# A two-layer encoder with expert retrieval: three token parts for tile 1, transposed token load, stationary gate weights, tile 0's v slots moved forward

## The chip, the cores and the metric

The kernel runs on one core of a Trainium2 chip. The metric is the device time of one execution in microseconds (us), the median of several.

## What is computed

The input is 256 tokens of 2048 floats. Layer 0 mixes tokens by attention and mLSTM heads that read one projection of the normalised tokens; layer 1 mixes by pooling. Each layer then has a PEER mixer, in which each token picks 128 of 16384 experts. Cut to what matters (`E` stands for the layer's output projection and residual, the routing is left out):

```python
hn = rmsnorm(h, norm_mix_g[layer])            # x * rsqrt(mean(x*x) + eps) * gain
proj = hn @ w_in                              # attention q, k, v; mLSTM q/k, v, output gate; 16 gate columns
# layer 1: pooled = windowed means of hn minus hn; y = pooled @ pool_w * layer_scale
xn = rmsnorm(h, norm_ffn_g[layer])
q = xn @ w_query; expert, gate = top16_of_pairs(q, sub_keys)      # 8 heads x 16 experts a token
act = gelu(einsum('tkd,td->tk', u[expert], xn))                   # 128 dots a token
h = h + einsum('tk,tkd->td', gate * act, v[expert])
```

The output is `rmsnorm(h, norm_f)`. All arithmetic is in float32.

## The kernel before

The tokens are two tiles of 128 (tile 0 and tile 1). Each engine has its own instruction stream, written out by hand, and waits on counting semaphores; so on each engine the order in the text is the order of the work, and a wait holds everything behind it.

**Mixer of layer 0.** SyncE (SP) loads the tokens, gains and constants, then the projection's weights in halves of 2 MiB through three slots (`load_half`). ScalarE (ACT) and VectorE (DVE) normalise a tile into `nrm0`, TensorE (PE) transposes it (`transpose_xn`), both evict it to `xnT`. `straight_half` multiplies `xnT` with a half; after the first half 32 matmuls with 16 moving columns make the gates (L1516), and small steps turn them into decays between the halves. Later halves use `xnT` as the moving operand (L1581).

**PEER, per layer.** The 128 experts of each token have their u rows gathered by GpSimd (POOL), one expert of each of 128 tokens at a time: 128 rows of 8 KiB, 1 MiB, into a ring of buffers (`gather_u`). A ring buffer is free again when VectorE has done its dot (`dot`, L1311: product and sum against the staged tokens in `low`). Tile 0 uses ring `U[0]` (a part of its rows goes to TensorE). Tile 1 is done in two halves of 64 tokens: in a half, the 128 partitions hold 64 tokens twice, with different experts (`idx_p`, made by the copies of L430 from `idx_all`), so each half takes 64 dots. TensorE stages the tokens of a half, doubled, in `low` (`duplicate`, L1823), which VectorE must have finished reading; for the second half this stands in TensorE's stream seven quads before the end of tile 0's spreading.

**From dots to weights.** ScalarE takes the gelu of a half when its dots are done (`gelu_half`, L787), VectorE multiplies with the gates (`weigh_half`, L1337, after the 13th dot of tile 1's fifth group of 16 for the first half), TensorE turns and folds it (`turn_half`). Then, for four tokens at a time (a quad), ScalarE builds two one-hot matrices (`one_hots`, L837 to L846), TensorE multiplies them (`spread`, L1837) and ScalarE copies the result to `W` (`spread_out`, L860). ScalarE does so for the 32 quads of tile 0, then for the 16 of tile 1's first half, both while the dots go on; the last 16 quads have their one-hots made by VectorE (L1370, L1374) after the last dot, and after every two of them TensorE adds one diagonal product of a v gather (`diagonal`, L1845): `ND` = 8 in all.

**v.** Half of v's columns are summed densely: 128 loads of 512 KiB (`load_vd`) against `W` (`dense`, L1858), in the banks of `low`. The other half is gathered: 128 rows of 4 KiB, 512 KiB (`gather_v`, L543), in eight slots. The order of the 256 gathers is the list `gathered`: first `ND` of tile 0, then tile 1 and tile 0 in turns, at the end the last of tile 1. The first 8 gathers go by slot, the next `ND` each wait for a diagonal, the others for VectorE's sums (`add_v`, L1351), which begin when the diagonals are added (`add_diagonals`). `pace` ties the dense loads to the sums.

**The boundary.** When the dense sums are done, SP loads the pooling matrix and its gains (L455, L456). VectorE takes the root of tile 0's norm and scales the pooling matrix with it (`mean_square`, `scale_pooling`, L958) near the end of its sums; TensorE pools tile 0, then tile 1 (L1870), then projects (L1772).

## Time and profile before

| | us |
|---|---|
| median of 3 runs | 3008.47 |
| lowest, highest | 3005.03, 3009.71 |
| the profiled execution | 3007.43 |
| its span in the profile | 3005.6 |

| engine | busy us | share |
|---|---|---|
| TensorE matmul | 2319.2 | 77% |
| VectorE | 2130.7 | 71% |
| ScalarE | 824.9 | 27% |
| GpSimd | 1081.7 | 36% |

DMA moved 1058.78 MB, 352 GB/s over the span. The page gives the mean busy share of the 16 DMA engines in 40 slices of 75 us as digits, tenths of full: `5333235899999999899999969999998999999999`. The first seven slices are the mixer of layer 0, the next sixteen the PEER of layer 0, the rest layer 1. A shares' column says which engine worked, not which one set the end; for that the timelines of one stretch are laid side by side, and in them the bracket behind an instruction tells how long its engine had been idle and what released it. Times in the rows count from the span's start.

### The profile page before, as it was taken

To read this page: it belongs to the slowest core of one execution; us is meant where nothing else is said; L and a number is where in the kernel's file an instruction comes from. 1 tells how busy PE (TensorE), PEld (TensorE's weight loads), DVE (VectorE), ACT (ScalarE), POOL (GpSimd) and SP (SyncE) were. 2 spreads that over 40 slices of the span, in tenths; PEclk is the share of its full clock that TensorE was granted. 3 is DMA by queue.
4 is the path that set the end of the run, shared out by engine and by line. 5 is a ranking of instruction groups with operands and counts; after the bars stand their busy time and mean duration, and the time that the engine had idled before them with its cause. 6 is when DMAs were issued, how large, how long until landed. Compare 5 with 4: busy or idle time off the path is not lost.

```text
span 3005.6 us, 26389 instructions
## 1 busy us (share of the span) xinstructions
PE 2319.2 (77%) x9174; PEld 1707.0 (57%) x9174; DVE 2130.7 (71%) x3110; ACT 824.9 (27%) x2109; POOL 1081.7 (36%) x1028
## 2 busy tenths in 40 slices
PE   8999999778873332799999888788443419999996
PEld 4686545677862332566665557778432316666654
DVE  1242122799999989856666768989998997566667
ACT  1242120112228986100000021212298941000000
POOL 0000000523334333444456624323333334444665
PEclk8999999889985555899999998999755559999998
DMA  5333235899999999899999969999999998999999
GB/s 215 140 112 140 112 116 234 344 413 412 390 389 420 421 416 421 301 410 409 409 409 409 409 265 417 408 411 378 388 421 416 417 420 293 410 409 409 409 409 360
DMA packets 196883, 1058.78 MB, mean 352 GB/s; under 512 B 23952, under 2 KB 24592, under 8 KB 123664
## 3 DMA queue, kind: packets, MB, share of 16 engines
q0 software_dynamic: 147456, 805.37, 66.1%
q1 hardware_dynamic: 49296, 251.74, 21.2%
q8 instruction: 73, 1.20, 0.2%
q14 instruction: 58, 0.48, 0.0%
HBM read 1054.53 MB, written 2.10 MB: 352 GB/s over the span
## 4 chain that ended last, share of the span: by engine, by line
DMA 45%; PE 27%; DVE 20%; issue 3%; POOL 3%; ACT 2%; DVEq 0%; SPq 0%; ACTq 0%; POOLq 0%
DMA arena<-pvg,idx_all 20%; DMA arena<-pu,ints 14%; DVE arena L1311 10%; DMA xnT<-pvg,idx_all 7%; PE bank L1496 7%; DMA arena<-pu,idx_all 4%; PE bank L1581 3%; DVE h L1351 3%; PE bank L1784 3%; PE bank L1733 2%; PE low L1698 2%; PE bank L1791 1%; PE bank L1837 1%; PE low L1687 1%; POOL xnT L543 1%
## 5 line engine op out<-in xcount | busy, mean ns | idle before, releaser
L1311 DVE CUSTOM_DVE_ANT_0 arena<-arena,low 128x2048 f32<-128x2048 f32 x418 | 944.5, 2285 | 93.0 <-DMA arena<-pu,ints 39.9
L1858 PE MATMUL low<-arena 128*128 128x512 f32 x2048 | 901.7, 600 | 31.2 <-DMA arena<-pvd 30.6
L1858 PEld LDWEIGHTS low<-arena 128*128 128x128 f32 x2048 | 601.6, 296 | 331.1 <-DMA arena<-pvd 68.5
L527 POOL DMA_INDIRECT arena<-pu,idx_all x200 | 222.7, 1113 | 862.5 <-DVE idx_all L1280 567.1
L1351 DVE SCALAR_TENSOR_TENSOR h<-arena,cst,h 128x1024 f32<-128x1024 f32 x248 | 318.0, 1285 | 163.8 <-DMA arena<-pvg,idx_all 163.1
L1351 DVE SCALAR_TENSOR_TENSOR h<-xnT,cst,h 128x1024 f32<-128x1024 f32 x248 | 317.6, 1285 | 163.5 <-DMA xnT<-pvg,idx_all 162.3
L1837 PE MATMUL bank<-arena 128*128 128x128 f32 x768 | 194.9, 434 | 294.5 <-ACT arena L846 294.5
L543 POOL DMA_INDIRECT arena<-pvg,idx_all x256 | 280.6, 1096 | 242.9 <-DVE h L1351 177.6
L543 POOL DMA_INDIRECT xnT<-pvg,idx_all x256 | 280.5, 1096 | 238.6 <-DVE h L1351 178.0
L1837 PEld LDWEIGHTS bank<-arena 128*128 128x128 f32 x768 | 167.8, 322 | 322.4 <-ACT arena L846 321.4
L569 ACT ACTIVATE h<-low 128x512 f32<-128x512 f32 x8 | 4.3, 589 | 938.6 <-PE low L1858 938.6
L1784 PE MATMUL bank<-xnT,arena 128*128 128x128 f32 x1792 | 244.7, 288 | 0.0
L837 ACT ACTIVATE arena<-cst,arena 128x128 f32<-128x128 f32 x768 | 233.7, 389 | 0.1
L1784 PEld LDWEIGHTS bank<-xnT,arena 128*128 128x128 f32 x1792 | 231.1, 202 | 0.0
L1733 PE MATMUL bank<-xnT,arena 128*128 128x256 f32 (+1 forms) x1152 | 218.0, 352 | 9.7 <-issue 5.7
L803 ACT ACTIVATE arena<-bank 128x512 f32<-128x512 f32 x224 | 133.8, 597 | 328.5 <-PE bank L1791 326.9
L1733 PEld LDWEIGHTS bank<-xnT,arena 128*128 128x128 f32 x1152 | 194.3, 197 | 31.1 <-issue 7.2
L1496 PE MATMUL bank<-arena,xnT 128*128 128x512 f32 x448 | 198.7, 600 | 2.0 <-issue 1.6
L506 POOL DMA_INDIRECT arena<-pu,ints x128 | 119.9, 936 | 207.6 <-DVE cst L1311 189.6
L527 POOL DMA_INDIRECT arena<-pu,ints x128 | 122.3, 956 | 189.0 <-DVE cst L1311 166.2
L1791 PE MATMUL bank<-cst,arena 128*128 128x128 f32 x608 | 102.0, 294 | 106.4 <-DVE cst L1320 71.5
L1496 PEld LDWEIGHTS bank<-arena,xnT 128*128 128x128 f32 x448 | 85.1, 193 | 102.6 <-issue 101.4
(256 smaller groups left out, 2182.6 us busy)
## 6 DMA issues: line engine op xcount, KB each, us to landing
arena<-pvd SPq DMA_DIRECT2D x256, 512.0 KB, 6.8
arena<-w_proj SPq DMA_DIRECT2D x22, 2048.0 KB, 7.8
arena<-wq SPq DMA_DIRECT2D x16, 2048.0 KB, 11.9
arena<-w_out SPq DMA_DIRECT2D x9, 2048.0 KB, 7.7
gB<-gains SPq DMA_DIRECT2D x4, 1024.0 KB, 10.1
arena<-pu,ints POOLq DMA_INDIRECT x256, 12.3
xnT<-pvg,idx_all POOLq DMA_INDIRECT x256, 13.8
arena<-pvg,idx_all POOLq DMA_INDIRECT x256, 13.9
```

The source lines that it names most:

```text
L527: nc.gpsimd.indirect_dma_start(U[t][slot], None, pu[L], bass.IndirectOffsetOnAxis(idx_p[:, d:d + 1] if t else row(n), 0)).then_inc(u_got[t ...
L543: nc.gpsimd.indirect_dma_start(vslots[m % VR], None, pvg[L], bass.IndirectOffsetOnAxis(idx_all[:, t * PH + hk // PK, hk % PK:hk % PK + 1], ...
L803: activation(UXT[i % 2][:, 4 * b:4 * b + 4], psum[4][:, :].rearrange("p (a b) -> p a b", a=4), ACT.Copy).then_inc(s["ux_ev"], 1)
L837: ins = activation(oh[:, b, i], iota, ACT.Square, scale=-1.0, bias=sT[:, x, t:t + 1])
L1311: vec.tensor_tensor_reduce(out=u, in0=u, in1=low[:, :] if staged else xns[0], scale=1.0, scalar=0.0, op0=ALU.mult, op1=ALU.add, accum_out= ...
L1351: vec.scalar_tensor_tensor(acc, vslots[m % VR], wv[:, t, hk:hk + 1], acc, ALU.mult, ALU.add).then_inc(s["vacc_done"], 1)
L1496: ins = mm(psum[4 + t][:, :], xnT[:, HALF * hf + k, t * P:(t + 1) * P], wslot[slot][:, k], start=hf == 0 and k == 0, stop=hf == 1 and k == ...
L1733: ins = mm(psum[6][:, p_ * S + t0 * P:p_ * S + t1 * P], wq_slots[slot][:, k, p_ * P:(p_ + 1) * P], xnT[:, k, t0 * P:t1 * P], start=k == 0, ...
L1784: ins = mm(psum[5][:, i % 4 * P:(i % 4 + 1) * P], UXT[i % 2][:, c], xnT[:, c, 0:P], start=c == 0, stop=c == KC - 1)
L1791: ins = tr(psum[4][:, x * P:(x + 1) * P], UX[i % UP][:, (4 * b + x) * P:(4 * b + x + 1) * P], ident)
L1837: ins = mm(psum[4 + q % 2][:, i * P:(i + 1) * P], o1[:, q % 2, i], o2[:, q % 2, i], start=True, stop=True)
L1858: ins = mm(psum[2 * t + c][:, 0:VH], W[t][:, :, n], vdense[:, n % DR, c * VH:(c + 1) * VH], start=False, stop=n == NK - 1)
```

## The change

What it does, in the order of the execution:

- The host gives the tokens transposed as well (`xt`), and the gain by chunk (`mix_gain`). SP loads half of `xt`, the first weight half, the gate weights, the other half of `xt`, the second weight half; then the tokens, the constants and the small arrays. VectorE multiplies the 16 chunks of `xnT` with the gain in place. There is no transposing before the first matmul. The norm's factor is applied where the first three weight columns are evicted (`evac_raw`, `scale=rs`) and to the gates; for what follows, VectorE multiplies `xnT` by the tokens' factors (`by_token`, two products after the fifth half and two after the sixth), which TensorE has laid out in a row.
- The gates: 16 matmuls with the 16 gate columns as the stationary operand and 256 moving columns, an eviction, two transposes after the second half. The decays' steps move one half back.
- Tile 1 is done in parts of 64, 32 and 32 tokens (`PARTS`). A part of 32 holds its tokens four times, with different experts, and takes 32 dots. There are ten copies of indices, of gates and of weights instead of four each. The rings have 7, 6 and 5 buffers (before 7 and 6); a sixth buffer lies where the one-hots were, and these go to `gB` for all quads. The staged tokens are replaced three times: for the third part after nine quads of tile 1. The first part is weighed behind tile 1's 73rd dot (before: 77th), the second behind its 105th, the third at the end.
- ScalarE makes the one-hots of the first 24 quads of tile 1, VectorE those of the last 8. There are four diagonals (`ND`).
- In `gathered` the last 16 entries are of tile 1 (before: 8), so tile 0's stand ahead. In layer 0 tile 0's root is taken 14 sums before the end and the pooling matrix scaled 13 before it (before: 4 and 3); the load of the pooling weights waits for five sums fewer than all (before: two).

```diff
-UT0, UT1, UT2, UP = 6, 7, 6, 3
+UT0, UT1, UT2, UT3, UP = 6, 7, 6, 5, 3
...
-LAST_T0 = 8
-ND, DG = 8, 2
+LAST_T0 = 16
+ND, DG = 4, 2
...
-HP = P // 2
-HQ = QUADS // 2
-NSEL = 2 * P + HP + 2
+PARTS = ((0, 64), (64, 32), (96, 32))
+NP = len(PARTS)
+LASTQ = PARTS[-1][0] // QT
+NSEL = NP * P + sum(w + P // w for _, w in PARTS[:2])
...
-        oh1 = carve(2, QT, P)
-        oh2 = carve(2, QT, P)
+        sixth = carve(D)
         fifth = carve(D)
...
-        U = [ring(0, UT0), ring(W_AT + P * P, 2) + [fifth] + ring(0, 4), [fifth] + ring(0, 4) + [xn1]]
+        U = [ring(0, UT0), ring(W_AT + P * P, 2) + [fifth] + ring(0, 4), [sixth, fifth] + ring(0, 4),
+             ring(0, 4) + [fifth]]
...
-        gathered = [(0, hk) for hk in range(ND)]
-        for i in range(HK - ND):
-            gathered += [(1, i), (0, ND + i)]
-        gathered += [(1, hk) for hk in range(HK - ND, HK)]
+        gathered = [(0, hk) for hk in range(LAST_T0)]
+        for i in range(HK - LAST_T0):
+            gathered += [(1, i), (0, LAST_T0 + i)]
+        gathered += [(1, hk) for hk in range(HK - LAST_T0, HK)]
...
-            sp.dma_start(h[:, 0, :], x[0:P, :]).then_inc(s["ld_x0"], 16)
-            gain(0)
-            sp.dma_start(cst[:], consts).then_inc(s["ld_c"], 16)
-            sp.dma_start(h[:, 1, :], x[P:S, :]).then_inc(s["ld_x1"], 16)
-            for i in range(2):
-                load_half(i, w_proj[i // 2, i % 2])
-            sp.dma_start(wg, w_gates.rearrange("p (k c) -> p k c", k=KC)).then_inc(s["ld_small"], 16)
+            def load_xt(hf):
+                cols = slice(HALF * S * hf, HALF * S * (hf + 1))
+                sp.dma_start(xnT_flat[:, cols], xt[:, cols]).then_inc(s[f"ld_t{hf}"], 16)
+
+            sp.dma_start(gT0, mix_gain).then_inc(s["ld_t0"], 16)
+            load_xt(0)
+            load_half(0, w_proj[0, 0])
+            sp.dma_start(wg, w_gates.rearrange("p (k c) -> p k c", k=KC)).then_inc(s["ld_t1"], 16)
+            load_xt(1)
+            load_half(1, w_proj[0, 1])
+            sp.dma_start(h[:, 0, :], x[0:P, :]).then_inc(s["ld_x0_pool0"], 16)
+            sp.dma_start(h[:, 1, :], x[P:S, :]).then_inc(s["ld_x1_pool1"], 16)
+            sp.dma_start(cst[:], consts).then_inc(s["ld_c_scale"], 16)
             sp.dma_start(bgB, b_gate.partition_broadcast(P)).then_inc(s["ld_small"], 16)
             sp.dma_start(cvw, conv_w).then_inc(s["ld_small"], 16)
             sp.dma_start(gB_q, q_gain.partition_broadcast(P)).then_inc(s["ld_small"], 16)
...
-                for hf in range(2):
-                    for pp, pc, op, oc in quadrants(hf):
+                for part in range(NP):
+                    for pp, pc, op, oc in blocks_of(part):
                         sp.dma_start(idx_p[pp, pc], idx1[op, oc]).then_inc(s["ld_idx"], 16)
                 sp.wait_ge(s["gates_ready"], L + 1)
-                for hf in range(2):
-                    for pp, pc, op, oc in quadrants(hf):
...
-                    sp.wait_ge(s["vacc_done"], NV - 2)
-                    sp.dma_start(poolw[:, 0].rearrange("p k c -> p (k c)"), pool_w[:, 0:D]).then_inc(s["ld_pool0"], 16)
...
-                    if d >= UT2:
-                        pool.wait_ge(s["dot_done"], base + HP + d - UT2 + 1)
-                    elif d == UT2 - 1:
-                        pool.wait_ge(s["dup_ready"], 2 * L + 2)
-                    else:
-                        pool.wait_ge(s["dot_done"], base + max(i for i in range(HP) if i % UT1 == d + 2) + 1)
+                    size, last = len(U[x]), PARTS[x - 2]
+                    if d >= size:
+                        pool.wait_ge(s["dot_done"], base + first + d - size + 1)
+                    elif u_place(x, d)[0] == 1:
+                        pool.wait_ge(s["dot_done"], base + last[0] + max(
+                            i for i in range(last[1]) if u_place(x - 1, i) == u_place(x, d)) + 1)
                     nc.gpsimd.indirect_dma_start(
-                        U[2][d % UT2], None, pu[L], bass.IndirectOffsetOnAxis(idx_p[:, HP + d:HP + d + 1], 0)
-                    ).then_inc(u_got[2][d % UT2], 16)
+                        U[x][d % size], None, pu[L], bass.IndirectOffsetOnAxis(idx_p[:, first + d:first + d + 1], 0)
+                    ).then_inc(u_got[x][d % size], 16)
                     return
                 if t == 0:
                     if d >= UT0:
...
-                    activation(dst, src, ACT.Copy).then_inc(s["raw_evac"], 1)
+                    if r < N_QKV:
+                        activation(dst, src, ACT.Copy, scale=rs[:, t:t + 1]).then_inc(s["raw_evac"], 1)
+                    else:
+                        activation(dst, src, ACT.Copy).then_inc(s["raw_evac"], 1)
 
             e.wait_ge(s["one_set"], 1)
             for t in range(TB):
                 norm(0, t)
-            for t in range(TB):
-                evac_xt(0, t)
-
+
+            e.wait_ge(s["gates_mm"], 1)
+            activation(gates_t[0:4 * MH], psum[6][0:4 * MH, 0:S], ACT.Copy).then_inc(s["gates_ev"], 1)
+            e.wait_ge(s["xn_ready"], TB)
+            evac_raw(0)
...
-                gelu_half(L, 0)
-                turned_half(L, 0)
-                for q in range(HQ):
-                    one_hots(L, QUADS + q)
-                    if q:
-                        spread_out(L, 1, q - 1)
-                spread_out(L, 1, HQ - 1)
-                gelu_half(L, 1)
-                turned_half(L, 1)
-                for q in range(HQ):
-                    if q % (HQ // ND) == 0:
-                        diagonal(L, q // (HQ // ND))
-                    spread_out(L, 1, HQ + q)
+                for part in range(NP - 1):
+                    gelu_part(L, part)
+                    turned_part(L, part)
+                    first, w = PARTS[part]
+                    for q in range(first // QT, (first + w) // QT):
+                        one_hots(L, QUADS + q)
+                        if q * QT > first:
+                            spread_out(L, 1, q - 1)
+                    spread_out(L, 1, (first + w) // QT - 1)
+                gelu_part(L, NP - 1)
+                turned_part(L, NP - 1)
+                for q in range(LASTQ, QUADS):
+                    if q % 2 == 0:
+                        diagonal(L, (q - LASTQ) // 2)
+                    spread_out(L, 1, q)
                 o = 2 + 2 * L
                 activation(root_load[:, 1 + L:2 + L], one, ACT.Sqrt)
                 add_dense(o, 0)
...
+            for k in range(KC):
+                if k % HALF == 0:
+                    v.wait_ge(s[f"ld_t{k // HALF}"], 32)
+                vec.tensor_scalar(xnT[:, k], xnT[:, k], gT0[:, k:k + 1], None, ALU.mult).then_inc(s["xt_ready"], 1)
...
+            by_token = rs_row.unsqueeze(1).to_broadcast([P, HALF // 2, S])
+            for c in range(4):
+                if c % 2 == 0:
+                    v.wait_ge(*((s["raw_done"], TB * N_QKV) if c else (s["w_used"], N_QKV)))
+                ks = xnT[:, c * HALF // 2:(c + 1) * HALF // 2]
+                ins = vec.tensor_tensor(ks, ks, by_token, ALU.mult)
+                if c % 2:
+                    ins.then_inc(s["xt_ready"], 1)
...
-                cols = slice(hf * HP, (hf + 1) * HP)
-                for b in range(2):
-                    ins = vec.scalar_tensor_tensor(w_p[:, hf, b * HP:(b + 1) * HP], act[:, 1, cols], of_half[:, b:b + 1],
+                first, w = PARTS[part]
+                cols = slice(first, first + w)
+                for b in range(P // w):
+                    ins = vec.scalar_tensor_tensor(w_p[:, part, b * w:(b + 1) * w], act[:, 1, cols], of_block[w][:, b:b + 1],
                                                    gates_p[:, cols], ALU.mult, ALU.mult)
                 ins.then_inc(s["w_ready"], 1)
 
...
                         if j == PH and k == 5:
                             weigh(L)
-                        if j == PH + PH // 2 and k == 12:
-                            weigh_half(L, 0)
-                weigh_half(L, 1)
-                for q in range(HQ, QUADS):
+                        if j == PH + PH // 2 and k == 8:
+                            weigh_part(L, 0)
+                        if j == PH + 3 * PH // 4 and k == 8:
+                            weigh_part(L, 1)
+                weigh_part(L, NP - 1)
+                for q in range(LASTQ, QUADS):
                     one_hots(L, q)
                 add_diagonals(L)
                 o = 2 + 2 * L
                 for j in range(NV):
                     add_v(L, j)
-                    if j == NV - 4:
+                    if j == NV - (4 if L else LAST_T0 - 2):
                         mean_square(o, 0)
-                    if j == NV - 3 and L == 0:
+                    if j == NV - LAST_T0 + 3 and L == 0:
                         scale_pooling(0)
...
-            pe.wait_ge(s["ld_c"], 16)
-            for t in range(TB):
-                transpose_xn(0, 0, t, nrm0[:, t])
-            pe.wait_ge(s["xt_act"], 4)
-            pe.wait_ge(s["xt_dve"], 4)
             straight_half(0, 0, 0)
-            pe.wait_ge(s["ld_small"], 6 * 16)
-            for t in range(TB):
-                for k in range(KC):
-                    ins = mm(psum[6][:, 4 * MH * t:4 * MH * (t + 1)], xnT[:, k, t * P:(t + 1) * P], wg[:, k],
-                             start=k == 0, stop=k == KC - 1)
+            pe.wait_ge(s["xt_ready"], KC)
+            for k in range(KC):
+                ins = mm(psum[6][0:4 * MH, 0:S], wg[:, k], xnT[:, k], start=k == 0, stop=k == KC - 1)
             ins.then_inc(s["gates_mm"], 1)
             straight_half(1, 0, 1)
 
+            pe.wait_ge(s["ld_c_scale"], 16)
+            pe.wait_ge(s["gates_ev"], 1)
+            for t in range(TB):
+                ins = tr(psum[7][:, 4 * MH * t:4 * MH * (t + 1)], gates_t[0:4 * MH, t * P:(t + 1) * P], ident[0:4 * MH, 0:4 * MH])
+            ins.then_inc(s["gates_tp"], 1)
+            straight_half(2, 1, 0)
             pe.wait_ge(s["lf_ready"], 1)
+            for t in range(TB):
+                mm(psum[7][:, P + t * P:P + (t + 1) * P], rs[:, t:t + 1].to_broadcast([P, P]), ident, start=True, stop=True)
             for t in range(TB):
                 for d, tri in enumerate((tri_f, tri_b)):
                     c = (2 * t + d) * MH
                     mm(psum[7][:, c:c + MH], tri, lf[:, t, d], start=True, stop=True)
                     ins = mm(psum[7][:, 16 + c:16 + c + MH], ones, lf[:, t, d], start=True, stop=True)
             ins.then_inc(s["cum_done"], 1)
-            straight_half(2, 1, 0)
+            straight_half(3, 1, 1)
 
             pe.wait_ge(s["scol_ready"], 1)
...
-                turn_half(L, 0)
-                for q in range(HQ):
+                turn_part(L, 0)
+                for q in range(PARTS[1][0] // QT):
+                    if q == 9:
+                        duplicate(L, 2)
                     spread(L, 1, q)
-                turn_half(L, 1)
-                for q in range(HQ):
-                    spread(L, 1, HQ + q)
-                    if q % (HQ // ND) == HQ // ND - 1:
-                        diagonal(L, q // (HQ // ND))
+                turn_part(L, 1)
+                for q in range(PARTS[1][0] // QT, LASTQ):
+                    spread(L, 1, q)
+                turn_part(L, 2)
+                for q in range(LASTQ, QUADS):
+                    spread(L, 1, q)
+                    if q % 2:
+                        diagonal(L, (q - LASTQ) // 2)
                 pe.wait_ge(s["spread_ev"], TB * QUADS * (L + 1))
                 for n in range(NK):
                     dense(L, n)
 def _selection(np):
 
```

`blocks_of(part)` gives the partition and column slices of the part's copies, `gelu_part`, `turned_part`, `weigh_part` and `turn_part` do for a part what the functions of a half did.

## Rows read from the trace of the kernel before

**Rows 1.** Windows of layer 0: busy us (instructions) by engine, TensorE clock, DMA share, GB/s.

```profile
1150.00:1200.00 50.00, 12.46 (x48) 10.70 (x48) 45.53 (x41) 28.84 (x83) 18.32 (x21) 0.50 1.01 422
1220.00:1270.00 50.00, 47.30 (x201) 33.20 (x202) 42.65 (x96) 13.57 (x27) 21.55 (x23) 0.94 0.71 246
1300.00:1350.00 50.00, 50.00 (x118) 34.36 (x117) 28.88 (x23) 0.00 (x0) 21.35 (x23) 1.00 1.03 410
```

**Rows 2.** VectorE's timeline around dot 64: start, us, line, operation [idle before <- released by].

```profile
1056.27 2.29 DVE L1311 CUSTOM_DVE_ANT_0 arena<-arena,low 128x2048 f32<-128x2048 f32 x1 [0.19 <-DMA arena<-pu,ints]
...
1064.35 2.29 DVE L1311 CUSTOM_DVE_ANT_0 arena<-arena,low 128x2048 f32<-128x2048 f32 x1 [5.79 <-PE low L1823]
...
1094.02 0.48 DVE L1337 SCALAR_TENSOR_TENSOR arena<-cst,arena 128x64 f32<-128x64 f32 x2 [0.87 <-ACT cst L787]
```

**Rows 3.** ScalarE's timeline: two one-hot groups four tokens apart, and part 0's last copy.

```profile
1065.63 2.43 ACT L837 ACTIVATE arena<-cst,arena 128x128 f32<-128x128 f32 x8
...
1070.79 2.43 ACT L837 ACTIVATE arena<-cst,arena 128x128 f32<-128x128 f32 x8
...
1180.13 0.60 ACT L860 ACTIVATE arena<-bank 128x512 f32<-128x512 f32 x1 [1.69 <-PE bank L1837]
```

**Rows 4.** The chain of waits in order of time: start, us, what.

```profile
162.33 3.46 PE bank L1581 x16
...
537.91 5.85 DMA arena<-pu,idx_all
```

**Rows 5.** VectorE's timeline: tile 1's last dot and the first v sums.

```profile
1217.30 2.29 DVE L1311 CUSTOM_DVE_ANT_0 arena<-arena,low 128x2048 f32<-128x2048 f32 x1 [0.21 <-DMA arena<-pu,ints]
...
1255.03 4.87 DVE L1351 SCALAR_TENSOR_TENSOR h<-xnT,cst,h 128x1024 f32<-128x1024 f32 x4
```

**Rows 6.** TensorE's timeline: the first and the last diagonal of layer 0.

```profile
1226.62 1.88 PE L1845 MATMUL bank<-xnT,cst 128*128 128x512 f32 x4
...
1251.79 1.88 PE L1845 MATMUL bank<-arena,cst 128*128 128x512 f32 x4
```

**Rows 7.** The index copies' line: count, ns min/median/max, first and last start.

```profile
L430 SPq DMA_DIRECT2D ints<-idx_all x8: 467/597/844, 881.2 to 2142.3; - x8
```

**Rows 8.** GpSimd's timeline: tile 1's first and third gathers.

```profile
888.16 0.93 POOL L527 DMA_INDIRECT arena<-pu,ints  x1 [1.36 <-DMA ints<-idx_all]
...
897.05 1.10 POOL L527 DMA_INDIRECT arena<-pu,ints  x1 [6.72 <-PE bank L1784]
```

**Rows 9.** SyncE's queue, two windows: first weight halves, pooling gains.

```profile
2.86 0.96 SPq L367 DMA_DIRECT2D arena<-w_proj  x2
...
1723.08 0.43 SPq L456 DMA_DIRECT2D cst<-pool_gain  x1
```

**Rows 10.** DMA issues of two short windows: count, KB each, us to landing.

```profile
arena<-w_proj SPq DMA_DIRECT2D x1, 2048.0 KB, 14.0
...
cst<-pool_gain SPq DMA_DIRECT2D x1, 8.0 KB, 8.8
```

**Rows 11.** TensorE's timeline at the start: first half, gates, second half.

```profile
21.94 13.97 PE L1496 MATMUL bank<-arena,xnT 128*128 128x512 f32 x32 [0.83 <-issue]
35.74 11.26 PE L1516 MATMUL bank<-arena,xnT 128*128 128x16 f32 x64
46.84 16.56 PE L1496 MATMUL bank<-arena,xnT 128*128 128x512 f32 x32
```

**Rows 12.** Windows of the start (columns as in rows 1).

```profile
0.00:18.00 18.00, 4.31 (x20) 3.70 (x20) 6.50 (x12) 7.09 (x11) 0.20 (x4) 1.00 0.90 370
39.00:45.00 6.00, 6.00 (x30) 6.00 (x29) 0.00 (x0) 0.00 (x0) 0.00 (x0) 0.50 0.56 238
```

**Rows 13.** VectorE's timeline at the boundary: last two sums, tile 1's scaling.

```profile
1735.69 2.67 DVE L1351 SCALAR_TENSOR_TENSOR h<-arena,cst,h 128x1024 f32<-128x1024 f32 x2
...
1740.38 0.50 DVE L958 TENSOR_SCALAR arena<-arena,stat 128x544 f32<-128x544 f32 x1
```

**Rows 14.** TensorE's timeline at the boundary: pooling of tile 0.

```profile
1735.92 6.52 PE L1870 MATMUL low<-arena,h 128*128 128x256 f32 x16 [13.25 <-DVE arena L958]
```

248 lines of the change are left out of this document (138 added, 110 removed).

## The prediction

> **What bounds the kernel now.** I read the page's slices first: DMA is at nine tenths or more through both PEER layers, except at three places in each, and TensorE is full in the mixer ahead of them. So the mixer goes by TensorE, a PEER layer by bytes, and in the layers only idle DMA time counts. The table of windows shows the rates: 422 GB/s while u rows are gathered, 410 while v rows are, and 246 in the 50 us around the last dot [rows 1]. The missing (410-246)*50/410 = 20.0 us are what the finer parts aim at. Then I read, around each switch, the timelines of VectorE, ScalarE and GpSimd side by side: the reader should see who is late there. A u row set is 1.049 MB, so DMA delivers one every 2.49 us; VectorE, when it has a backlog, takes 2.21 us for one (13 dots from 1064.35 to 1094.02-0.87) [rows 1, 2]. So VectorE has only 0.28 us per dot to catch up, about 36 us over tile 1's 128 dots. Last come the start and the boundary between the layers, where the chain of waits is on TensorE and VectorE.
>
> **The order of steps at tile 1 (layer 0's times; layer 1 repeats them).** Dot 64 of tile 1 ends at 1056.27+2.29 = 1058.6; TensorE overwrites the staged tokens, and dot 65 starts at 1064.35 [rows 2]. ScalarE builds tile 0's one-hots meanwhile, and only then does tile 1's first gelu: VectorE, behind dot 77, waits 0.87 us for it, until 1094.02 [rows 2]. ScalarE needs 5.16 us for four tokens, and its 64 tokens of part 0 are done at 1180.13+0.60 = 1180.7 [rows 3].
>
> **The first switch, moved from dot 77 to dot 73.** It changes nothing of ScalarE's schedule, so the gelu still comes just before 1094.02. But VectorE now stands at the wait after 9 dots, at 1064.35+9*2.21 = 1084.2, and stays until 1094.0: 9.8 us, with four dots behind it that it had done in that time. DMA holds six buffers. From 1058.6 on they are all asked for (the new sixth buffer is free early), DMA lands the last it may land, number 79, 14 periods after number 65: 1058.8+34.9 = 1093.6. The products (0.48 us) and a dot (2.21) later, at 1097.0, the next gather is issued; from its issue to the first data I take 5.85-2.49 = 3.4 us, by a gather that met an idle DMA [rows 4], so DMA idles until 1100.4: 6.8 us.
>
> **The second switch, new.** VectorE reaches dot 96 at 1096.6+22*2.21 = 1145.2, with TensorE waiting for it after nine quads of tile 1. Overwriting the staged tokens again costs the 5.8 us seen at 1058.6 [rows 2]; DMA, with five buffers now, runs dry for about 2 us. Nine dots later, at 1170.8, VectorE waits for the gelu of part 1, and that stands behind ScalarE's sixteen quads, at 1180.7. With 0.3 us of gelu and four small products instead of two (0.24 us each [rows 2]) it goes on at 1182.0. 105 dots are done and 23 are left: 23*2.21 = 50.8 us, so the last dot can't end before 1232.8. By DMA it is later: the next gather is issued at 1182.0+2.2+0.4 = 1184.6, brings data from 1188.0, and 18 are due, 18*2.49 = 44.8: 1232.8, and a dot behind it, 1235.1. Now the last dot ends at 1217.30+2.29 = 1219.6 [rows 5]. **So the dots end 15.5 us later** (13.2 by VectorE alone).
> Part 1's eight quads cost ScalarE 8*5.16 = 41.3 us from about 1183.5, until 1225: hidden by the dots, with 10 us to spare.
>
> **The tail.** From the last dot to the first v sum it is 1255.03-1219.6 = 35.4 us now [rows 5]. In it are eight rounds of eight tokens and one diagonal; first and last diagonal start at 1226.62 and 1251.79, so a round is 25.17/7 = 3.60 us [rows 6]. Four rounds go: -14.4 us. The two more products cost +0.5. So the v sums begin 15.5-13.9 = +1.6 us later than now. What lies ready by then is less: with four diagonals instead of eight, 12 v gathers are on their way and not 16, so 4*0.524 MB more are left to a saturated DMA, 2.1/0.410 = 5.1 us. **A layer: +6.7 us.** Bounds: +4.4 when only VectorE limits the dots, +9 if a new gather takes 4.5 instead of 3.4 us to its first data at both restarts.
> Ten index copies replace four. SP issues one in 0.60 us (median), four from 881.2 on, and the first gather of tile 1 leaves at 888.16, the third, which waits for TensorE, at 897.05 [rows 7, 8]. Six more copies: 3.6 us, the first gather leaves at about 892 and, with the second, is landed (3.4+5.0 us) when the third brings data at 900.4. I take 0, bounds 0 and +3.6 a layer. In layer 1 the end has the same order of steps as now. The ten gate copies and eight more unfolding ones have tens of us to spare on SP, whose only followers are the v loads that wait for the last dot.
> The Trainium skill (DMA: Bandwidth & Descriptors, Rules for kernel authors) says to coalesce small transfers, and that two transfers to disjoint partition halves serialize rather than help; it speaks against the ten copies. Weighed against the rows: by the rule the 3.6 us are simply paid, +7.2 over both layers and 3019 in all; by the rows no engine of the chain waits for them.
>
> **The start.** The first weight half is issued at 2.86 and lands 14.0 us later, at 16.9 [rows 9, 10], the last of 5.56 MiB (two of tokens, one of gains, 0.56 of constants, two of weights); at 2.49 us per MiB the stream began at 3.1. With one MiB of transposed tokens and the two of weights ahead it lands at 3.1+7.5 = 10.6; VectorE's scaling of a chunk adds 0.3. TensorE starts at 11.0 instead of 21.94 [rows 11]: -10.9. Its first matmuls will be at the low clock, since nothing ran before them: the same 32 records took 13.97 us and, after the slow gate stage, 16.56 [rows 11]: +2.6. The gate product is 16 matmuls with 256 moving columns; eight of such took 3.46 us, so 6.9 instead of 46.84-35.74 = 11.1: -4.2 [rows 4, 11]. If TensorE keeps its clock through it (now the clock is 0.50 there [rows 12]), the next half takes 13.97: -2.6. The two turns back and the two root rows, which the trace has no match for, are some four matmuls of 128 columns: +0.8 (0 to 1.5). **Sum -14.3**, bounds -16.9 (no slow start) and -4.8 (rival 3). The norm's roots need only be there for the first eviction, some 25 us after the tokens land; the two pairs of products on the transposed tokens are 0.7 us per 512 elements each, finished long before chunk 8 is read. The chain of the gates now has a whole half (14 us) to hide in. TensorE stays the bound to 530 us, so the gain arrives whole.
> In the profile's clock column the first 18 us, with the first transposes, stand at 1.00, and the fast records only follow later [rows 12]. The Trainium skill (TensorE: Matmul & The Clock Gate, What's actually happening) has the slow clock as the default that activity releases. By it the 2.6 us hold; by the column alone the start would gain 16.9.
>
> **The layers' boundary.** VectorE's steps for tile 0's root now stand 14 sums before the end and the scaling of the pooling matrix 13 before it. The first waits for the dense sums, the second for the matrix and its gains, which are asked for only when the dense sums are done; the gains land at 1723.08+8.8 = 1731.9 [rows 9, 10]. Queued behind the waits are the last 13 sums, which now end at 1735.69+2.67 = 1738.4 [rows 13]. One goes between the waits; twelve follow from about 1731 (a little sooner than now, since fewer v gathers compete with the load): 12*1.28 = 15.4, end 1746.5, 8.1 later. TensorE's pooling of tile 0 starts 4 us sooner (1732 instead of 1735.92 [rows 14]), but tile 1's scaling, done at 1740.9 now [rows 13], comes at 1749. Now TensorE is busy with tile 0 for 5 us beyond that scaling (a first half of 6.5 us, a second of some 3.5, until 1746 [rows 14]). So tile 1 is late by 8.1-5 = +3 us, and TensorE, idle for 7 us before it, will be at the low clock again, as it was from 1735.92: +2. **+5**, bounds -4 (the sums are not held up) and +8.
>
> **Sum**: -14.3+6.7+5+6.7 = +4.1. The profiled execution took 3007.4 (span 3005.6 and 1.8 around it); the median is 1.0 above it. 3007.4+4.1+1.0 = 3012.5, so **3012**.
>
> **Rivals.** (1) The waits are absorbed, the last dot stays at DMA's pace, and the tail gives its full 13.9 us: 13.9-5.1 = 8.8 a layer, 3008.5-14.3-17.6+5 = 2982. For it: the deeper ring at the first switch. Against it: ScalarE's times, which no edit moves, and 23 dots of 2.21 us after 1182. Chance 0.12. (2) The boundary gains its 4 us and TensorE starts at the high clock: 3012-9-2.6 = 3000. For it: the clock column. Against it: the order of VectorE's queue. Chance 0.14. (3) Slower: the gate product fills only 16 columns of the array, and TensorE stays at the low clock through it, as it does in the gate stage now [rows 12]. Then it takes 13.8, not 6.9, and the next half keeps its 2.6: +9.5, 3021. It decides from the point where the product's granted clock is under 1. Against it: 256 columns stream where 16 did. Chance 0.14. (4) The forecast, 0.60, its own range 3003 to 3020.
>
> **How the numbers follow.** About 0.2% (6 us) is what a measurement can tell from no change: 3002.5 to 3014.5. Faster: 0.12 of (1), 0.12 of (2), 0.01 of (4): 0.25. Same: 0.02 of (2) and 0.39 of (4): 0.41. Slower: 0.14 of (3), 0.20 of (4): 0.34. The range reaches from rival (2)'s neighbourhood, with the boundary's and a layer's lower bounds, to (3)'s with a layer's upper ones: 2994 to 3024. It leaves out (1) and a little above.
>
> **What would show it.** First long TensorE matmul near 11 us, gate stage near 7 us, end of the raw projections 14 us sooner. VectorE idle for about 10 us before the small products of part 0 and of part 1 with ScalarE named, DMA under 300 GB/s in the slices there; last dot of tile 1 about 177 us after dot 64, not 161. From last dot to first v sum about 21 us. VectorE idle before the scaling of the pooling matrix. If the two waits are short, or the last dot comes within 163 us of dot 64, the forecast is wrong toward (1).

## The result and the profile after

The changed kernel took 3026.61 us (median of 4, 3023.23 to 3029.27), the kernel before on the same chip 3009.01: ratio 1.0063, 95% interval 1.0047 to 1.0079. It is slower by 0.6%, and lies above the range (2994 to 3024) of the prediction. The profiled execution took 3024.12. Its page:

```profile
span 3022.3 us, 26469 instructions
PE 2323.9 (77%) x9104; PEld 1700.6 (56%) x9104; DVE 2116.5 (70%) x3066; ACT 895.2 (30%) x2326; POOL 1111.3 (37%) x1028
PEclk9999999889975555899999999999755558999998
DMA  6323243999999998999999969999999989999998
```

VectorE's dots and v sums are the landmarks of a layer, so I read the two traces there. First come three lines of VectorE's timeline before: first dot, first dot of tile 1, first dot of layer 1 (the others stand in [rows 2, 5, 13]).

```profile
519.72 2.29 DVE L1311 CUSTOM_DVE_ANT_0 arena<-arena 128x2048 f32<-128x2048 f32 x1 [7.93 <-DMA arena<-pu,idx_all]
...
900.36 2.29 DVE L1311 CUSTOM_DVE_ANT_0 arena<-arena,low 128x2048 f32<-128x2048 f32 x1 [0.80 <-PE low L1823]
...
1788.78 2.29 DVE L1311 CUSTOM_DVE_ANT_0 arena<-arena 128x2048 f32<-128x2048 f32 x1
```

The same timeline after: first dot, first dot of tile 1, dot 64, last dot, first v sum, last v sums, first dot of layer 1.

```profile
505.66 2.29 DVE L1359 CUSTOM_DVE_ANT_0 arena<-arena 128x2048 f32<-128x2048 f32 x1 [9.26 <-DMA arena<-pu,idx_all]
...
887.71 2.29 DVE L1359 CUSTOM_DVE_ANT_0 arena<-arena,low 128x2048 f32<-128x2048 f32 x1 [0.99 <-DMA arena<-pu,ints]
...
1046.93 2.29 DVE L1359 CUSTOM_DVE_ANT_0 arena<-arena,low 128x2048 f32<-128x2048 f32 x1 [0.19 <-DMA arena<-pu,ints]
...
1225.99 2.29 DVE L1359 CUSTOM_DVE_ANT_0 arena<-arena,low 128x2048 f32<-128x2048 f32 x1 [0.20 <-DMA arena<-pu,ints]
...
1250.38 2.67 DVE L1401 SCALAR_TENSOR_TENSOR h<-arena,cst,h 128x1024 f32<-128x1024 f32 x2
...
1741.78 5.45 DVE L1401 SCALAR_TENSOR_TENSOR h<-arena,cst,h 128x1024 f32<-128x1024 f32 x4
...
1795.94 2.29 DVE L1359 CUSTOM_DVE_ANT_0 arena<-arena 128x2048 f32<-128x2048 f32 x1
```

A stretch runs from one landmark to the next; layer 1's come from the same view. The two spans differ by 16.7 us, and this is where they come from:

| stretch | before | after | more | forecast |
|---|---|---|---|---|
| to the first dot | 519.72 | 505.66 | -14.1 | -14.3 |
| layer 0, tile 0's dots | 380.64 | 382.05 | +1.4 | 0 |
| tile 1, first dot to end of dot 64 | 158.20 | 161.51 | +3.3 | 0 |
| end of dot 64 to end of last dot | 161.03 | 179.06 | +18.0 | +15.5 |
| last dot to first v sum | 35.44 | 22.10 | -13.3 | -13.9 |
| v sums | 483.33 | 496.85 | +13.5 | +13.2 |
| to layer 1's first dot | 50.42 | 48.71 | -1.7 | -3.1 |
| layer 1, tile 0's dots | 370.91 | 367.34 | -3.6 | 0 |
| tile 1, first dot to end of dot 64 | 159.05 | 161.11 | +2.1 | 0 |
| end of dot 64 to end of last dot | 160.79 | 179.98 | +19.2 | +15.5 |
| last dot to first v sum | 36.92 | 22.35 | -14.6 | -13.9 |
| v sums | 480.19 | 486.67 | +6.5 | +5.1 |
| to the end | 8.96 | 8.91 | -0.1 | 0 |

(Forecast of the v sums of layer 0: 5.1 for fewer rows on their way and 8.1 for the sums held up; the 5 of the boundary less 8.1 is the line below it.) The stretch of tile 0's dots varies from one execution to another: between 378.2 and 385.8 us in layer 0 and 366.8 and 373.7 in layer 1 over all the kernels here, though no edit of the experiments touches it. Its +1.4 and -3.6 mean nothing. The stretches behind it repeat within 1 to 2 us.

The start, TensorE's timeline after: first half of the weights, gates, second half.

```profile
11.45 15.82 PE L1550 MATMUL bank<-arena,xnT 128*128 128x512 f32 x32 [11.45 <-DMA arena<-w_proj]
27.20 7.08 PE L1564 MATMUL bank<-xnT,arena 128*16 128x256 f32 x32
34.21 14.00 PE L1550 MATMUL bank<-arena,xnT 128*128 128x512 f32 x32
```

First matmul at 11.45 (11.0 was worked out), first half 15.8 us where the second takes 14.0, gates 7.1 (6.9): the terms of the start hold, and rival 3 is out. Two windows of it (TensorE's busy time and count stand first, its granted clock behind the five engines):

```profile
13.00:14.00 1.00, 1.00 (x2) 0.34 (x1) 0.00 (x0) 0.00 (x0) 0.00 (x0) 1.00 1.20 508
18.00:19.00 1.00, 1.00 (x4) 0.43 (x3) 0.00 (x0) 0.00 (x0) 0.00 (x0) 1.00 0.92 385
```

The counts take in matmuls that an edge cuts: two touch the first microsecond, four the second. From start to start it is 0.85 us (the first time 1.02) up to the fifth matmul, at 15.03, and 0.43 us behind it: half the pace, though the clock column says 1.00 for both. The trace has no record of the clock before 15.14 us (in the trace of before none ahead of 14.51), and where there is none the column reads 1.00. The slow beginning costs 1.8 us, not 2.6.

The switches, VectorE's timeline after. The reader should look at the brackets: 9.69 us for ScalarE before part 0's products, 6.28 for the restaged tokens, 8.66 for ScalarE before part 1's.

```profile
1072.56 0.08 DVE L1359 DVE_READ_ACCUMULATOR2_ANT cst<- 128x1 f32 x1
...
1084.54 0.48 DVE L1386 SCALAR_TENSOR_TENSOR arena<-cst,arena 128x64 f32<-128x64 f32 x2 [9.69 <-ACT cst L813]
...
1143.01 2.29 DVE L1359 CUSTOM_DVE_ANT_0 arena<-arena,low 128x2048 f32<-128x2048 f32 x1 [6.28 <-PE low L1880]
...
1172.64 0.74 DVE L1386 SCALAR_TENSOR_TENSOR arena<-cst,arena 128x32 f32<-128x32 f32 x4 [8.66 <-ACT cst L813]
1173.29 2.28 DVE L1359 CUSTOM_DVE_ANT_0 arena<-arena,low 128x2048 f32<-128x2048 f32 x1
```

ScalarE's timeline: gelu of tile 0, of part 0, last group of part 0, gelu of part 1. Part 1's gelu comes 88.1 us behind part 0's, at once after the copy of the last group.

```profile
900.66 0.40 ACT L806 ACTIVATE cst<-cst,stat 128x128 f32<-128x128 f32 x1
...
1084.26 0.25 ACT L813 ACTIVATE cst<-cst 128x64 f32<-128x64 f32 x1
...
1171.89 0.60 ACT L887 ACTIVATE arena<-bank 128x512 f32<-128x512 f32 x1 [1.69 <-PE bank L1893]
1172.38 0.22 ACT L813 ACTIVATE cst<-cst 128x32 f32<-128x32 f32 x1
```

ScalarE itself waits behind the dots at two places. TensorE restages tokens only when VectorE has done the last dot that reads them, and ScalarE's next copy waits for what TensorE does behind the restaging: 11.25 us behind dot 64 (10.19 before), and 1.16 us behind dot 96, for which TensorE waits 2.44 us (ScalarE, TensorE, ScalarE):

```profile
1055.67 0.60 ACT L887 ACTIVATE arena<-bank 128x512 f32<-128x512 f32 x1 [11.25 <-PE bank L1893]
...
1136.87 5.99 PE L1880 MATMUL low<-arena 128*128 128x512 f32 x8 [2.44 <-DVE cst L1359]
...
1143.79 0.60 ACT L887 ACTIVATE arena<-bank 128x512 f32<-128x512 f32 x1 [1.16 <-PE bank L1893]
```

And the windows there (the last number of a line is GB/s): 287 at the first wait, 350 at the restaging, 277 at the second wait, 422 and 401 between and behind them. Before, the windows from 1080 to 1200 us hold 420 to 422.

```profile
1070.00:1090.00 20.00, 7.24 (x28) 6.17 (x28) 10.31 (x13) 16.61 (x49) 3.75 (x4) 0.50 0.72 287
1120.00:1140.00 20.00, 9.35 (x28) 6.85 (x29) 16.16 (x16) 19.87 (x60) 6.57 (x7) 0.50 1.01 422
1140.00:1160.00 20.00, 9.35 (x39) 6.91 (x38) 16.99 (x15) 18.71 (x54) 6.56 (x7) 0.67 0.91 350
1160.00:1180.00 20.00, 7.13 (x30) 6.11 (x29) 10.42 (x15) 16.68 (x51) 3.74 (x4) 0.50 0.69 277
1180.00:1200.00 20.00, 8.11 (x33) 6.93 (x33) 19.21 (x17) 19.87 (x60) 8.43 (x9) 0.50 1.00 401
```

The copies of tile 1's indices (SP) and the gathers behind them (GpSimd):

```profile
868.43 6.36 SPq L449 DMA_DIRECT2D ints<-idx_all  x10
...
873.09 0.94 POOL L548 DMA_INDIRECT arena<-pu,idx_all  x1 [1.27 <-DVE cst L1359]
881.36 1.75 POOL L548 DMA_INDIRECT arena<-pu,ints  x1 [7.34 <-DMA ints<-idx_all]
883.41 1.91 POOL L548 DMA_INDIRECT arena<-pu,ints  x1 [0.30 <-issue]
```

Ten copies are issued in 6.36 us and the first gather of tile 1 leaves 13 us after the first of them; before, it left 7 us after it (from 881.2 to 888.16 [rows 8]). Now it waits 7.34 us for the copies, and the first three go out in a row.

Layer 0's end, VectorE's timeline after, shows 9.48 us of idle time ahead of the root, 0.99 ahead of the scaling, and twelve sums behind it.

```profile
1727.40 0.15 DVE L974 TENSOR_SCALAR stat<-stat 128x1 f32<-128x1 f32 x1 [9.48 <-ACT arena L584]
...
1727.67 1.28 DVE L1401 SCALAR_TENSOR_TENSOR h<-xnT,cst,h 128x1024 f32<-128x1024 f32 x1
...
1730.02 0.75 DVE L987 TENSOR_SCALAR arena<-arena,stat 128x1024 f32<-128x1024 f32 x1 [0.99 <-DMA cst<-pool_gain]
1730.68 5.44 DVE L1401 SCALAR_TENSOR_TENSOR h<-arena,cst,h 128x1024 f32<-128x1024 f32 x4
...
1741.78 5.45 DVE L1401 SCALAR_TENSOR_TENSOR h<-arena,cst,h 128x1024 f32<-128x1024 f32 x4
```

TensorE's pooling of tile 0, and of tile 1 after 9.52 us without work:

```profile
1730.91 5.93 PE L1926 MATMUL low<-arena,h 128*128 128x256 f32 x16 [6.88 <-DVE arena L987]
...
1749.82 4.00 PE L1926 MATMUL low<-arena,h 128*128 128x136 f32 x16 [9.52 <-DVE arena L987]
```

### The profile page after: what moved, and what is told of

Read it like the earlier page. It is cut to its first block, busy times and chain, and to the rows that moved or that the text cites. A ratio compares the mean times of both kernels' runs of the same rounds, so it can differ in the third digit from the quotient of the medians.

```text
span 3022.3 us, 26469 instructions
## 1 busy us (share of the span) xinstructions
PE 2323.9 (77%) x9104; PEld 1700.6 (56%) x9104; DVE 2116.5 (70%) x3066; ACT 895.2 (30%) x2326; POOL 1111.3 (37%) x1028
## 4 chain that ended last, share of the span: by engine, by line
DMA 43%; DVE 24%; PE 21%; POOL 4%; ACT 4%; issue 3%; SPq 0%; DVEq 0%; POOLq 0%; ACTq 0%
DMA xnT<-pvg,idx_all 18%; DVE arena L1359 13%; DMA arena<-pu,ints 12%; DMA arena<-pvg,idx_all 7%; PE bank L1550 6%; DMA arena<-pu,idx_all 5%; DVE h L1401 3%; PE bank L1637 3%; PE low L1754 2%; ACT gB L864 2%; POOL arena L564 1%; POOL xnT L564 1%; POOL arena L548 1%; PE bank L1893 1%; PE low L1743 1%
## 5 line engine op out<-in xcount | busy, mean ns | idle before, releaser
L1914 PE MATMUL low<-arena 128*128 128x512 f32 x2048 | 905.2, 601 | 37.3 <-DMA arena<-pvd 36.7
L1893 PE MATMUL bank<-gB 128*128 128x128 f32 x1024 | 243.4, 415 | 341.7 <-ACT gB L873 337.4
L1401 DVE SCALAR_TENSOR_TENSOR h<-arena,cst,h 128x1024 f32<-128x1024 f32 x256 | 328.6, 1285 | 164.9 <-DMA arena<-pvg,idx_all 161.0
L1893 PEld LDWEIGHTS bank<-gB 128*128 128x128 f32 x1024 | 211.8, 307 | 376.9 <-ACT gB L873 367.5
L564 POOL DMA_INDIRECT xnT<-pvg,idx_all x256 | 294.4, 1150 | 226.2 <-DVE h L1401 168.1
L564 POOL DMA_INDIRECT arena<-pvg,idx_all x256 | 296.3, 1158 | 215.6 <-DVE h L1401 174.1
L864 ACT ACTIVATE gB<-cst,arena 128x128 f32<-128x128 f32 x896 | 272.6, 389 | 0.2
## 6 DMA issues: line engine op xcount, KB each, us to landing
arena<-pu,idx_all POOLq DMA_INDIRECT x238, 11.8
```

The costliest lines, as they stand in the source:

```text
L564: nc.gpsimd.indirect_dma_start(vslots[m % VR], None, pvg[L], bass.IndirectOffsetOnAxis(idx_all[:, t * PH + hk // PK, hk % PK:hk % PK + 1], ...
L864: ins = activation(oh[:, b, i], iota, ACT.Square, scale=-1.0, bias=sT[:, x, t:t + 1])
L1401: vec.scalar_tensor_tensor(acc, vslots[m % VR], wv[:, t, hk:hk + 1], acc, ALU.mult, ALU.add).then_inc(s["vacc_done"], 1)
L1893: ins = mm(psum[4 + q % 2][:, i * P:(i + 1) * P], oh1[:, q % 2, i], oh2[:, q % 2, i], start=True, stop=True)
L1914: ins = mm(psum[2 * t + c][:, 0:VH], W[t][:, :, n], vdense[:, n % DR, c * VH:(c + 1) * VH], start=False, stop=n == NK - 1)
```

## The experiments

Each kernel is timed against the kernel before on the same chip; the stretches are those of the table. Where two values stand for a stretch, they are layer 0's and layer 1's.

### Part 1's products later

```diff
-                        if j == PH + 3 * PH // 4 and k == 8:
+                        if j == PH + 6 and k == 12:
```


> The changed kernel with one step moved: VectorE's small products for part 1 stand behind dot 109 of tile 1 and not behind dot 105. Theory A (ScalarE's sixteen one-hot groups set when part 1 can be weighed, and dots queued behind that wait are lost): in the changed kernel dot 105 ends at 1163.98 and the next starts at 1173.29; with four dots ahead of the wait VectorE arrives at about 1172-1173 and waits under 2 us, the last dot ends 23*2.49 = 57.3 us after dot 105, at 1221.3 instead of 1228.3: 7.0 us a layer, 14 over both, so about 3012.5 (ratio to before 1.0015). The groups of part 1 start no later, since the gelu sets them. Rival B (the loss lies in the four fewer v gathers in flight, in the copies of the indices and at the boundary, and the dots' delay is made up by a longer queue of transfers): no change, 3026.


Ratio 1.0027 (1.0016 to 1.0038), 3013.6 us. From dot 64 to the last dot 174.3 and 171.1 us instead of 179.1 and 180.0. No wait for ScalarE is left at the new place in either layer; what VectorE waits for in layer 0 is a gather, 1.7 us ahead of dot 109. By the stretches 13.6 us over both layers, 14 expected (by the ratios 0.0036, 10.8 us): theory A holds.

### Part 0's products back

```diff
-                        if j == PH + PH // 2 and k == 8:
+                        if j == PH + PH // 2 and k == 12:
```


> The changed kernel with VectorE's small products for part 0 back behind dot 77 (they stand behind dot 73). Theory A (the second wait ends last): the first wait shrinks from 10.2 to about 1.4 us and DMA loses no time there, but part 1's gelu still comes at about 1173, nine dots behind dot 96, which VectorE now reaches some 8 us sooner; the wait there grows from 9.3 to about 17 us and the last dot ends where it did: 0 to -2 us in all, 3025 to 3027. Rival B (each wait costs its own idle DMA time, 6.8 us at the first): -13.6 over both layers, 3013.


Ratio 1.0056 (1.0044 to 1.0068). The wait of 9.7 us and its idle DMA time are gone: dot 96 ends 6.0 and 6.7 us sooner. The last dot ends 178.9 and 178.6 us after dot 64, -0.2 and -1.4: VectorE's gap behind dot 105 grew from 9.31 to 13.57. Two waits for one late engine don't add up; the second takes nearly all that the first gives. What changes for ScalarE is small: part 1's gelu comes 86.9 us behind part 0's here, not 88.1 and 88.5, since TensorE no longer waits for dot 96. Theory A holds.

### Both

```diff
-                        if j == PH + PH // 2 and k == 8:
+                        if j == PH + PH // 2 and k == 12:
-                        if j == PH + 3 * PH // 4 and k == 8:
+                        if j == PH + 6 and k == 14:
```


> The changed kernel with part 0's small products behind dot 77 (not 73) and part 1's behind dot 111 (not 105). Theory A (ScalarE's groups set the time of part 1's gelu; what is lost is the dots that stand behind the wait, and once they don't, the first wait's 10 us count as well): moving the first alone gave 2 us and the second alone 11 to 14; together the dots run at DMA's pace but for TensorE's restaging, VectorE waits under 2 us at either place, the last dot ends about 168 to 170 us after dot 64 instead of 179, and the whole is 20 to 24 us under the changed kernel: ratio to before about 0.9985. Rival B (the two add up and no more): 13 to 16 us, 1.0015.


Ratio 1.0002 (0.9993 to 1.0010), 3005.6: 18.3 us under the changed kernel's ratio (0.0061 of 3005), more than the sum of the two, less than expected. The stretch is 169.7 and 167.9, together 21.4 us less, where the two moves alone gave 13.6 and 1.6. Now the restaging shows (VectorE, then TensorE, layer 0):

```profile
1123.58 2.29 DVE L1359 CUSTOM_DVE_ANT_0 arena<-arena,low 128x2048 f32<-128x2048 f32 x1 [0.19 <-DMA arena<-pu,ints]
...
1136.09 2.29 DVE L1359 CUSTOM_DVE_ANT_0 arena<-arena,low 128x2048 f32<-128x2048 f32 x1 [10.22 <-PE low L1880]
...
1128.33 2.08 PE L1893 MATMUL bank<-gB 128*128 128x128 f32 x8 [3.09 <-ACT gB L873]
1130.19 5.75 PE L1880 MATMUL low<-arena 128*128 128x512 f32 x8
```

Dot 96 ends at 1125.9, TensorE begins to restage at 1130.19 only: in its fixed order a group of part 0 comes first, and that group waits for ScalarE.

### One switch, moved alone

This is the kernel with two parts of 64 tokens (the next experiment), with its only switch four dots sooner.

```diff
-                        if j == PH + PH // 2 and k == 12:
+                        if j == PH + PH // 2 and k == 8:
```


> The kernel with the new start and two parts of 64 (measured at 0.9969 of before), with the one switch behind dot 73 instead of 77. No second wait follows here that could hide the first. Theory A (a dot that stands behind a wait for ScalarE is idle DMA time, as the prediction worked out): VectorE waits 9.8 us there, DMA idles 6.8, and the stretch from dot 64 to the last dot goes from 161.8 to 168.6 us in layer 0: 13 to 14 us over both layers, ratio 1.001 to 1.0015. Rival B (six buffers and VectorE's faster pace take it back within the 55 dots left): stretch at 162 to 164, ratio 0.9975.


Ratio 1.0010 (1.0000 to 1.0020) against 0.9969. Stretch 169.5 us in both layers instead of 161.8 and 160.9: +7.7 and +8.6; 6.8 was worked out from rows of before. VectorE's timeline and the windows around it:

```profile
1066.99 0.08 DVE L1358 DVE_READ_ACCUMULATOR2_ANT cst<- 128x1 f32 x1
...
1078.97 0.48 DVE L1385 SCALAR_TENSOR_TENSOR arena<-cst,arena 128x64 f32<-128x64 f32 x2 [9.69 <-ACT cst L812]
...
1062.00:1082.00 20.00, 7.90 (x32) 6.54 (x30) 10.31 (x13) 16.57 (x50) 3.83 (x5) 0.50 0.80 333
1082.00:1102.00 20.00, 7.28 (x29) 6.39 (x30) 20.00 (x19) 19.87 (x60) 8.55 (x10) 0.50 0.92 349
```

With two parts the windows hold 425 and 417 GB/s, so (92+68)*20/422 = 7.6 us of DMA time are missing, the whole of it. Theory A holds.

### Two parts of 64: the start alone

```diff
-PARTS = ((0, 64), (64, 32), (96, 32))
+PARTS = ((0, 64), (64, 64))
-LAST_T0 = 16
-ND, DG = 4, 2
+LAST_T0 = 8
+ND, DG = 8, 2
-                        if j == PH + PH // 2 and k == 8:
+                        if j == PH + PH // 2 and k == 12:
-                        if j == PH + 3 * PH // 4 and k == 8:
-                            weigh_part(L, 1)
...
-                    if q == 9:
-                        duplicate(L, 2)
...
-                turn_part(L, 2)
```


> The changed kernel with two parts of 64 tokens instead of 64, 32 and 32: switch behind dot 77, eight diagonals, eight tile 0 slots among the last gathers, four index copies; the start is the new one, the steps for the root stand at 6 and 5 sums before the end. Theory A (the start is worth 14, the rest of the loss is the parts, the copies and the boundary): first u gather 15 us sooner than before, 13 left at the first dots of tile 1, and kept by the last dot, its tail 35 us as before; at the boundary 1 to 3 us are given back: about 2998 (ratio 0.9965). Rival B (what the start gains is lost again in the layers, whatever the parts are, since DMA sets their pace): 3006 to 3009.


Ratio 0.9969 (0.9958 to 0.9980), 2995.0. Faster than before: the start's 14 us arrive (first dot of tile 1 at 885.45, before 900.36), and 3.7 are given back in layer 0's v sums (486.99). With ten copies gone, the stretch to dot 64 is 158.02. Theory A holds. Besides the start this kernel keeps the sixth buffer, the root's steps two sums sooner than before and the early request for the pooling weights.

### The root's steps back

```diff
-                    if j == NV - (4 if L else LAST_T0 - 2):
+                    if j == NV - 4:
-                    if j == NV - LAST_T0 + 3 and L == 0:
+                    if j == NV - 3 and L == 0:
```


> The changed kernel with VectorE's two steps for tile 0's root in layer 0 back at 4 and 3 sums before the end (they stand 14 and 13 before it). Theory A (twelve sums are queued behind the wait for the pooling gains): the sums end about 8 us sooner, TensorE's pooling of tile 1 starts 3 us sooner and at the high clock, and the span is 5 to 6 us shorter: 3021 (ratio 1.0043). Rival B (the boundary is late because the last v rows come later, by the four fewer gathers in flight): no change, 3026; the steps' place doesn't matter.


Ratio 1.0055 (1.0043 to 1.0067). Layer 0's v sums take 490.6 us and not 496.9, the stretch behind them 48.3 (48.7): 6.6 us, as theory A has it. The ratios show less of it (0.0008, 2.4 us), within their intervals.

With two parts of 64, where the steps stood 6 and 5 before the end, the same edit:


> The same kernel with two parts of 64 and the root's steps of layer 0 at 4 and 3 sums before the end, where they stood in the kernel before (here 6 and 5): only the new start is left of the change, with the sixth buffer. Theory A (the parts of 32, even placed well, give back in the restaging, the copies and the four fewer v rows in flight what the shorter tail saves; the best kernel so far owes its lead over two parts of 64 to the root's place): the v sums of layer 0 go from 487 to 483.5 us, ratio 0.9955 to 0.996, within 2 us of the combined kernel. Rival B (the parts of 32 are worth some 6 us when placed well): 5 us or more above the combined kernel's time.


Ratio 0.9960 (0.9947 to 0.9973). The ratio is the expected one, but the v sums stay at 486.9 and don't fall to 483.5: two sums' difference of place cost nothing, so something else takes 3.6 us there. What remained was the request for the pooling weights:

```diff
-                    sp.wait_ge(s["vacc_done"], NV - 5)
+                    sp.wait_ge(s["vacc_done"], NV - 2)
```


> The kernel with two parts of 64 and the root's steps in their old place, with the pooling weights asked for behind sum NV-2, as before the change, and not NV-5. Theory A (the early 2 MB and more of weights take DMA time from the last v rows): the v sums of layer 0 go from 486.9 back to 483.5 us, the stretch from their end to layer 1's first dot from 45.8 to 50 us; the whole 0 to +2 us. Rival B (the weights' place is free for the sums): the sums stay at 487.


Ratio 0.9961 (0.9948 to 0.9973). The sums take 483.4, as before the change, and the stretch behind them 50.6 (45.8 with the early request): both as theory A says, +1.4 together. The early request thus moves 3.5 us into the sums and takes 4.8 from behind them.

### The index copies

```diff
-sp.dma_start(idx_p[pp, pc], idx1[op, oc]).then_inc(s["ld_idx"], 16)
+sp.dma_start(idx_p[pp, pc], idx1[op, oc]).then_inc(s["ld_idx2" if part else "ld_idx"], 16)
-                    pool.wait_ge(s["ld_idx"], 16 * N_BLOCKS * (L + 1))
+                    pool.wait_ge(s["ld_idx"], 32 * (L + 1))
...
+                    if x == 2 and d == 0:
+                        pool.wait_ge(s["ld_idx2"], 16 * (N_BLOCKS - 2) * (L + 1))
```


> The changed kernel with the ten copies of tile 1's indices split over two semaphores: the first gather of tile 1 waits for the two copies of part 0 alone, the eight others are waited for at part 1's first gather. Theory A (the copies are paid on the path: from the first dot of tile 1 to the end of dot 64 it takes 161 to 162 us in the three kernels with ten copies that gather so, and 158.1 in the two with four): that stretch goes to 158 us or a little under, 3.3 us less a layer, 6.6 in all: about 0.22% off the changed kernel's ratio (1.0063), 1.0041. Rival B (the three microseconds are something else in that stretch, the larger ring or the places of the buffers): the stretch stays at 161.5.


Ratio 1.0062 (1.0049 to 1.0075): no gain, 1.0041 expected. GpSimd's first gathers of tile 1:

```profile
875.11 0.94 POOL L550 DMA_INDIRECT arena<-pu,ints  x1 [1.83 <-DMA ints<-idx_all]
876.35 0.94 POOL L550 DMA_INDIRECT arena<-pu,ints  x1 [0.30 <-issue]
884.32 2.46 POOL L550 DMA_INDIRECT arena<-pu,ints  x1 [7.03 <-PE bank L1842]
```

They leave 7.4 us after the first copy now, and the stretch to dot 64 is 160.3 us in both layers (161.5, 161.1): 1.2 and 0.8 back, not 3.3. So the first gather's wait for all ten copies accounts for less than half of it. The gate weights' ten copies, right behind, were the next suspect:

```diff
                 sp.wait_ge(s["gates_ready"], L + 1)
+                sp.wait_ge(s["dot_done"], L * NDOT + ND0 + 40)
```


> The changed kernel with the index copies split over two semaphores and, besides, the ten copies of the gate weights held on SP until dot 40 of tile 1 (they ran right behind the index copies, while the first gathers of tile 1 were asked for). Theory A (the ten small copies compete with the first gathers): the stretch from the first dot of tile 1 to the end of dot 64 goes from 160.3 to 158 to 158.5 us. Rival B (the rest of the loss is not in SP's copies; the gathers of tile 1 come as late by TensorE's last turned row): it stays at 160.3.


The stretch is 159.0 and 160.0 us, between the two theories. Over all kernels and both layers it is 158.0 to 160.3 with four copies (median of ten 158.7) and 160.8 to 162.6 with ten unsplit (median of twelve 161.4): the kernels with ten copies pay 2.7 us there. The kernels that split them, with the two of the next but one section, have 158.1 to 160.7 (median of eight 159.8), so the split brings back some 1.6 of it. The delay of the gate weights isn't told apart from their spread, and the rest is left open.

The whole gains nothing by it. In the split kernel the gap behind dot 105 grew from 9.31 to 10.33 and the way from dot 64 to the last dot to 181.7 and 181.4. With the gate weights held back that way is 178.5 and 180.4, so tile 1's dots are 3.1 and 0.7 us shorter in all, but tile 0's dots, the stretch that varies, took 3.8 and 4.3 more: 1.0060 (1.0048 to 1.0072).

### Eight diagonals

```diff
-ND, DG = 4, 2
+ND, DG = 8, 2
...
-                    if q % 2 == 0:
-                        diagonal(L, (q - LASTQ) // 2)
+                    diagonal(L, q - LASTQ)
```


> The changed kernel with eight diagonals, one for each of the last part's eight groups, instead of four. Theory A (a gathered v row more taken by TensorE is one more on its way, but each diagonal costs TensorE 1.9 us in a tail that TensorE sets): the v sums of a layer take 6.5 us less (487 to 480 in layer 1), the stretch from the last dot to the first sum 7 us more (22 to 29): between -1 and +2 us a layer, 3026 to 3029. Rival B (the tail is set by VectorE's one-hot groups, diagonals are hidden beside them): the tail stays at 22 to 24 and the whole gains 10 to 13 us, 3014.


Ratio 1.0072 (1.0060 to 1.0084). Tail 28.9 and 28.2 us (22.1, 22.4), v sums 491.3 and 481.3 (496.9, 486.7): +6.8 and -5.6, +5.8 and -5.4. The four rows fewer on their way are what the v sums lose in the changed kernel, and a diagonal costs as much as it brings. Theory A holds.

### All together

Both switches as above, the restaging before group 8, index copies split, the root's steps back.


> The changed kernel with all that the runs so far speak for: part 0's small products behind dot 77, part 1's behind dot 111, TensorE's second restaging before group 8 of tile 1 and not before group 9, the index copies split in two, the root's steps of layer 0 back at 4 and 3 sums before the end. Theory A: terms as above, -22 for the switches, -6.6 for the copies, -6.2 for the root's place, some -2 for the restaging: about 37 us under the changed kernel, 2987 to 2990, ratio 0.993, under both kernels and under the one with two parts of 64 (0.9969). Rival B (with the waits gone DMA is the bound throughout, and the copies' and the root's gains are hidden by it): 2998 to 3002, no better than two parts of 64.


Ratio 0.9950 (0.9937 to 0.9963), 2990.9: under the kernel before by 0.5%, and 6 us short of the ratio that was expected. 64 to last dot 166.7 and 163.0 us; two parts of 64 have 161.8 and 160.9. Against these, by the stretches of layer 0, the parts of 32 give 13.6 in the tail (23.2, 36.7) and give back 4.9 up to the last dot and 4.7 in the v sums; in layer 1 10.5 in the tail against 2.1 and 6.8. The stretches to dot 64 and the one behind the sums take another 4.5, so that some 1 us is left of it all. The lead over two parts of 64 with the root's steps in their old place (0.9960) is 0.001, within the intervals, as theory A of that run has it.

```diff
-                        if j == PH + 6 and k == 14:
+                        if j == PH + 7 and k == 0:
```


> The combined kernel (0.995 of before) with part 1's small products behind dot 113 and not 111: VectorE waited 3.75 us for ScalarE at the place in layer 1, and not at all in layer 0. Theory A: the wait of layer 1 goes under 1 us and 1 to 2 us are gained, 0.9945. Rival B (TensorE's groups of part 1 now start later and the tail begins later by as much): no change, 0.995.


Ratio 0.9972 (0.9961 to 0.9984): worse, as rival B has it and by more. The dots end sooner (165.3 us after dot 64 in layer 0), but the tail takes 29.4 and 29.1 us. Its head on VectorE:

```profile
1206.11 2.29 DVE L1361 CUSTOM_DVE_ANT_0 arena<-arena,low 128x2048 f32<-128x2048 f32 x1 [0.23 <-DMA arena<-pu,ints]
...
1216.00 0.74 DVE L1388 SCALAR_TENSOR_TENSOR arena<-cst,arena 128x32 f32<-128x32 f32 x4 [7.59 <-ACT cst L815]
```

VectorE waits 7.59 us for the gelu of part 2, which stands behind ScalarE's eight groups of part 1. ScalarE is the limit of the parts of 32: it makes 56 groups of four tokens at 5.16 us a layer where two parts give it 48, and with the products this late the last part waits for its last group.

## Why the prediction was wrong

**The first switch** held: 9.8 us of waiting were worked out, 9.69 measured; 6.8 us of idle DMA, 7.6 measured where it stands alone. The sum rightly didn't add the idle time to the second one (the experiment with part 0's products back). But "It changes nothing of ScalarE's schedule" was wrong: VectorE reaches dot 96 late by the wait, TensorE waits 2.44 us for it before restaging, and ScalarE's copy behind that is late. Part 1's gelu comes 88.1 to 89.3 us behind part 0's in both layers of all six kernels with three parts and the products behind dot 73, and 86.9 in the four with the products behind dot 77.

Rival 1 (the waits are absorbed) is out with these waits, and rival 2 (the boundary gains) with the 9.48 us of idle time at the root.

**The second switch** held in its mechanism, not in its size, and is one of two steps that failed. "So the dots end 15.5 us later": 18.0 and 19.2. In layer 0 part 1's gelu came 88.1 us after part 0's, not 87.0 (1180.7 less 1093.7), by the lateness just told, and from the dot behind the wait to the end of the last it took 55.0 us, not 53.1. The restaging of dot 96, put down at about 2 us of DMA time, shows (422-350)*20/422 = 3.4 in its window. In the sum it lay under the wait behind it; set free, it costs 2 to 5 us (from dot 96 to the last 85.2 and 82.4 in the combined kernel, 79.9 and 80.4 with two parts), and more while TensorE's order holds it back (88.5).

**The index copies** are the other step that failed: "I take 0, bounds 0 and +3.6 a layer". The stretch they stand in is 3.3 and 2.1 us longer. The working said when the first gather leaves ("about 892", the measured 881.36 plus the 14 us of the start is 895) and then let the first two land under cover of TensorE's third. That overlooked that all ten copies are waited for at once, and that GpSimd issues gathers one after another: the first three go out at 881.36, 883.41 and 885.62 now, so the second dot starts 3.28 us behind the first (2.21 before) and the tenth 24.0 us behind it (20.9). With the copies split the second dot is back at 2.21 and the tenth at 22.2, and still the stretch keeps the larger part of its loss: what the rest is stays open. The row of the copies' issue carried about the right price.

The Trainium skill (DMA: Bandwidth & Descriptors, Rules for kernel authors) says to coalesce small transfers. By that rule the prediction's sum would have been 7.2 us more; the trace agrees in direction, with 5.4 more.

The loss up to dot 64 is passed on whole. Tile 0's gelu comes later too (12.95 us behind the first dot of tile 1, 11.14 before), but ScalarE waits again for TensorE behind dot 64, and there its schedule is tied to the dots: in both layers of all fifteen kernels part 0's gelu comes 34.8 to 36.4 us behind the end of dot 64, 35.2 in layer 0 before and 35.0 after.

**The tail** held: -13.3 and -14.6 for -13.9. **The rows on their way** cost 6.5 in layer 1 for 5.1. **The boundary** held as a whole, with the rows on their way: 13.5-1.7 = 11.8 for 10.1. Its parts did not: the place of the root's steps costs 6.2 us in the sums and 0.4 behind them (8.1 and -3.1 were worked out). The gain behind the sums comes from a part that was left out, the earlier pooling weights; measured, they put 3.5 us into the sums and take 4.8 from behind them. **The start** held to 0.2 us.

Added up, the forecast of +4.1 misses: copies 5.4, second switch 6.2, sums and boundary 3.1, tile 0's varying dots -2.2, start and tail 0.1: 12.6, and 4.1+12.6 = 16.7. Without the copies' 5.4, or without the second switch's 6.2, the time would have been inside the range. The range's upper end was rival 3's 3021 with a layer's upper bound, and the copies' "+3.6" stood in neither end. Even both upper bounds in both layers, 3012.5+4.6+7.2 = 3024.3, stay under the measured 3026.6.

## What to carry to other kernels

A switch that waits for an engine which is late anyway should stand in the program where that engine arrives, and not sooner: every item queued behind the wait is a transfer not asked for. Finer parts of a hand-over shorten the tail only if the engine that makes them has the time; count its items (56 for 48 here) before counting the tail. An engine that is delayed on purpose can be what a third engine waits for: here VectorE's wait held TensorE's restaging, and that held ScalarE, for which VectorE was waiting. Where several small copies share one semaphore with the first thing that is needed, they are on the path, whatever covers that thing alone; here splitting them brought back some 1.6 of 2.7 us.

## What the runs showed of the hardware

TensorE's first matmuls, up to 15.03 us, started 0.85 us apart and the later ones 0.43, while the clock column stood at 1.00: the clock records begin at 15.14 us only, so for the beginning the spacing of the records tells the clock and the column doesn't. A gather's issue takes GpSimd 0.94 us, but 1.04 to 2.98 for one to three of the first gathers of tile 1; behind one of 0.94 the next can follow at 1.24. Ten small copies take SP 6.36 us to issue. When the pooling weights are asked for three sums sooner, 3.5 us move into the sums and 4.8 out of the stretch behind them, and the ratio stays (0.9960 and 0.9961). And tile 0's dots, the same work in each kernel, differ by 7 us from one execution to another; half a per cent in such a kernel is read from stretches, not from totals.
